# Up projection of the feed-forward part: 4 plain pairs of tiles, then 18 pairs by Strassen's seven products

## The reference

```python
def conv_ffn(h, w_up, conv_w, conv_b, w_down):     # D_FF = 2816, w_up is 1024 x 5632, w_down 2816 x 1024
    u = h @ w_up
    u_pad = jnp.pad(u, ((0, 0), (2, 0), (0, 0)))
    u = conv_b + conv_w[0] * u_pad[:, 0:s] + conv_w[1] * u_pad[:, 1:1 + s] + conv_w[2] * u_pad[:, 2:2 + s]
    gate, val = u[..., :D_FF], u[..., D_FF:]
    return (jax.nn.silu(gate) * val) @ w_down
# x = x + conv_ffn(rms_norm(x), ...), then a last rms_norm
```

## Time and profile before

| | us |
|---|---|
| three runs, median (lowest to highest) | 2477.18 (2477.11 to 2480.08) |
| profiled execution, its own time | 2477.57 |
| its span, first to last instruction | 2476.0 |
| TensorE busy | 2448.7 (99%), 11696 matmuls |
| VectorE busy | 1416.4 (57%) |
| ScalarE busy | 805.5 (33%) |

### The profile page before, as it was taken

The page is one execution under the profiler, slowest core; times in us unless marked ns, Lnnn a source line. Parts: engine busy times, 40 slices in busy tenths (PEclk is TensorE's granted clock), DMA queues, the critical chain, the costliest instruction groups (busy, mean ns, idle before and its releaser), DMA issues.

```text
span 2476.0 us, 31910 instructions
## 1 busy us (share of the span) xinstructions
PE 2448.7 (99%) x11696; PEld 2035.2 (82%) x11696; DVE 1416.4 (57%) x2288; ACT 805.5 (33%) x1513; POOL 95.4 (4%) x112
## 2 busy tenths in 40 slices
PE   8999999999999999999999999999999999999998
PEld 6888888888888888887788888988888888888876
DVE  5747887777532242435555743563677257734775
ACT  5334545444521131222233243452322112211224
POOL 1000000000000000021000030012000000000000
PEclk9999999999999999999999999999999999999999
DMA  5111111111111131221110142451111111111123
GB/s 198 35 43 52 43 52 50 45 51 52 51 51 43 50 119 47 80 85 48 42 47 22 30 141 85 132 192 51 43 51 51 44 50 51 48 46 51 46 62 122
DMA packets 236404, 160.97 MB, mean 65 GB/s; under 512 B 5295, under 2 KB 223572, under 8 KB 235299
## 3 DMA queue, kind: packets, MB, share of 16 engines
q1 hardware_dynamic: 229456, 132.66, 17.9%
q0 software_dynamic: 4976, 18.75, 2.2%
q10 hardware_dynamic: 1890, 8.43, 1.1%
HBM read 138.85 MB, written 20.97 MB: 65 GB/s over the span
## 4 chain that ended last, share of the span: by engine, by line
PE 97%; DVE 1%; DMA 1%; ACT 0%; issue 0%; SPq 0%; ACTq 0%; DVEq 0%
PE bank L716 26%; PE bank L717 26%; PE bank L718 26%; PE bank L1050 1%; PE bank L871 1%; PE bank L1051 1%; PE bank L1052 1%; PE bank L1247 1%; PE bank L1249 1%; PE bank L1248 1%; PE bank L1103 1%; PE bank L1104 1%; PE bank L1102 1%; DMA wraw<-in_w_in_dram 1%; PE bank L883 1%; PE bank L882 1%
## 5 line engine op out<-in xcount | busy, mean ns | idle before, releaser
L716 PE MATMUL bank<-xhi,whi 128*128 128x512 f32 x1056 | 411.8, 390 | 0.5 <-DVE wlo L1861 0.5
L717 PE MATMUL bank<-xlo,whi 128*128 128x512 f32 x1056 | 411.0, 389 | 0.0
L718 PE MATMUL bank<-xhi,wlo 128*128 128x512 f32 x1056 | 411.0, 389 | 0.0
L1861 DVE TENSOR_TENSOR wlo<-wraw,whi 128x1024 fp32r<-128x1024 f32 (+1 forms) x240 | 285.2, 1188 | 149.3 <-ACT whi L1281 99.8
L1288 ACT ACTIVATE whi<-wraw 128x1024 fp32r<-128x1024 f32 x132 | 139.3, 1056 | 573.2 <-PE bank L718 569.3
L716 PE MATMUL bank<-x4hi,whi 128*128 128x512 f32 x704 | 274.3, 390 | 0.0
L718 PE MATMUL bank<-x4hi,wlo 128*128 128x512 f32 x704 | 273.9, 389 | 0.0
L717 PE MATMUL bank<-x4lo,whi 128*128 128x512 f32 x704 | 273.9, 389 | 0.0
L716 PEld LDWEIGHTS bank<-xhi,whi 128*128 128x128 f32 x1056 | 198.3, 188 | 42.7 <-DVE wlo L1861 0.7
L717 PEld LDWEIGHTS bank<-xlo,whi 128*128 128x128 f32 x1056 | 198.3, 188 | 41.5 <-issue 0.2
L718 PEld LDWEIGHTS bank<-xhi,wlo 128*128 128x128 f32 x1056 | 198.3, 188 | 41.1
(11 more groups left out here) (397 smaller groups left out, 4507.2 us busy)
## 6 DMA issues: line engine op xcount, KB each, us to landing
wraw<-in_w_in_dram SPq DMA_DIRECT2D x85, 512.0 KB, 3.8
wraw<-in_ffn_w_up_dram SPq DMA_DIRECT2D x44, 512.0 KB, 3.7
wraw<-in_xattn_wkv_dram SPq DMA_DIRECT2D x16, 512.0 KB, 4.0
wraw<-in_ffn_w_down_dram SPq DMA_DIRECT2D x16, 512.0 KB, 3.9
wraw<-in_ffn_w_down_dram SPq DMA_DIRECT2D x16, 384.0 KB, 3.4
xraw<-in_x_dram SPq DMA_DIRECT2D x4, 1024.0 KB, 10.2
x_spill<-xt SPq DMA_DIRECT2D x8, 512.0 KB, 2.8
conv_spill<-tv POOLq DMA_DIRECT2D x8, 512.0 KB, 3.1
```

Of the source, the lines that this page charges most:

```text
L716: pe.matmul(acc, whi[slot][:, k, :], xh, start=(k == 0), stop=False)
L717: pe.matmul(acc, whi[slot][:, k, :], xl, start=False, stop=False)
L718: last = pe.matmul(acc, wlo[slot][:, k, :], xh, start=False, stop=(k == k_tiles - 1))
L1861: dve.tensor_tensor(wlo[slot][:, 0:n, :], wraw[slot][:, 0:n, :], whi[slot][:, 0:n, :].bitcast(F32), ALU.subtract).then_inc(s_wlo, 1)
```

## The change

The first 4 pairs stay plain matmuls. For each of the other 18, the product of [gate tile; value tile] with [tokens 0 to 511, tokens 512 to 1023], contraction in two halves of 4 blocks, is a product of 2 x 2 blocks, a11 a12 (gate), a21 a22 (value) by b11 b12, b21 b22, and is made with seven block products instead of eight (Winograd's form of Strassen):

- the weights' sums s1 = a21 + a22, s2 = s1 - a11, s3 = a11 - a21, s4 = a12 - s2 are made for each pair by VectorE (`weight_sum`), and seven high and low parts by ScalarE and VectorE (`weight_hi`, `weight_lo`) instead of two of double size;
- the input's sums t1 to t4 are made once, between the plain pairs (`t_forms`: terms on ScalarE, sums and low parts on VectorE);
- each product is 4 blocks x 3 matmuls of 512 columns. A pair uses three banks, x, y and z (`FORM_BANKS`: 4, 5, 6 or 0, 1, 2 in turn). ScalarE copies bank x to bank y before y is accumulated further (`y_begin`), copies y out (`copy_v`), and again (`copy_u3`); VectorE sums c12, c22 and takes c11, c21 times R.

Other parts: the first tap and SiLU move to ScalarE (`tap0`, `silu`). f tiles no longer stay in SBUF: each is stored to DRAM as it is made (`store_f`) and loaded again (`load_f`), and its two parts made then (`f_hi`, `f_lo`). All 22 pairs come first, then 8 + 8 down tiles, then the last 8 by half as before. The first down tile stands in banks 6 and 7. Some semaphores are shared.

```diff
+PLAIN = 4
+T_DN = T_FF + 2 * PLAIN
+T_LAST = T_DN + 16
+WEIGHT_ORDER = ("a11", "s1", "a12", "s2", "s3", "a22", "s4")
...
+            def next_pair(p, stored=None, last=False):            # SP
+                sp.wait_ge(s_as, 4 * p + 4)
+                sp.wait_ge(s_alo, 7 * p + 3)
...
+                    load_gate(p + 1)
+                if stored is not None:
+                    store_f(stored)
+                sp.wait_ge(s_alo, 7 * p + 6)
...
+                    load_value(p + 1)
...
+            for r, done in enumerate((2, 3, 5, 7)):
+                sp.wait_ge(s_m, 7 * LASTP + done)
+                for n in (2 * r, 2 * r + 1):
...
+                    load_f(n)
...
+            def form_step(p, q, first=False, last=False):         # TensorE
+                form_product("s1", "t1", "z", p, q)
+                pe.wait_ge(s_cp, 3 * p + 1)
+                form_product("s2", "t2", "y", p, q)
+                form_product("a12", "b21", "x", p, q)
+                pe.wait_ge(s_cp, 3 * p + 2)
+                form_product("s3", "t3", "y", p, q)
+                if not last:
+                    if not first:
+                        pe.wait_ge(s_c, 4 * p - 2)
+                    form_product("a11", "b11", "x", p + 1, 1 - q)
+                pe.wait_ge(s_cp, 3 * p + 3)
+                form_product("a22", "t4", "y", p, q, 2 if last else 1)
+                pe.wait_ge(s_c, 4 * p + 1)
+                form_product("s4", "b22", "z", p, q)
...
+            def first_down_tile():
...
+                for ks in (range(0, 6), range(6, 8)):
+                    for h in range(2):
+                        for k in ks:
+                            pe.wait_ge(s_ffn_lo, k + 1)
...
+            def form_step(p, q, first=False, last=False):         # ScalarE
+                weight_hi("s4", p)
+                if not last:
+                    weight_hi("a11", p + 1)
+                if not first:
+                    taps_of(p - 1)
+                copy_v(p, q)
+                if not last:
+                    weight_hi("s1", p + 1)
+                    weight_hi("a12", p + 1)
+                if not first:
+                    silu(p + (PLAIN - 1), 2)
+                if not last:
+                    weight_hi("s2", p + 1)
+                else:
+                    f_hi(0)
+                    f_hi(1)
+                copy_u3(p, q)
+                if not last:
+                    weight_hi("s3", p + 1)
+                    y_begin(p + 1, 1 - q)
+                    weight_hi("a22", p + 1)
...
+            def form_step(p, q, first=False, last=False):         # VectorE
+                n = p + (PLAIN - 1)
+                if not first:
+                    c12(p - 1, 1 - q)
+                    normed_hi(p - 1)
+                weight_lo("s4", p)
+                if not last:
+                    weight_lo("a11", p + 1)
+                if not first:
+                    taps(n, uv, yv, FF_TILES, 1)
+                if not last:
+                    weight_sum("s1", p + 1)
+                if not first:
+                    taps(n, ug, yg, 0, 2)
+                if not last:
+                    weight_sum("s2", p + 1)
+                    weight_lo("s1", p + 1)
+                    weight_sum("s4", p + 1)
+                    weight_lo("a12", p + 1)
+                else:
+                    f_lo(0)
+                    f_lo(1)
+                c22(p, q)
+                if not last:
+                    weight_sum("s3", p + 1)
+                    weight_lo("s2", p + 1)
+                if not first:
+                    product(n)
+                if not last:
+                    weight_lo("s3", p + 1)
+                else:
+                    f_lo(2)
+                    f_lo(3)
+                    split(T_DN, T_DN % 2)
+                    split(T_DN + 1, (T_DN + 1) % 2)
+                c11_c21(p, q)
+                if not last:
+                    weight_lo("a22", p + 1)
+                else:
+                    f_lo(4)
+                    f_lo(5)
...
+            def copy_u3(p, q):                                    # ScalarE
+                act.wait_ge(s_m, 7 * p + 5)
+                act.wait_ge(s_tap, 2 * p + (2 * PLAIN - (0 if isinstance(p, int) and p == 0 else 1)))
+                act.activation(uv[:, 2 + HALF:2 + S], ps(FORM_BANKS[q]["y"]), ACT.Copy).then_inc(s_cp, 1)
...
+            def c11_c21(p, q):                                    # VectorE
+                dve.wait_ge(s_m, 7 * p + 7)
...
-                        order.link(conv(i, yv, FF_TILES + done, h * HALF, HALF))
-                        dve.wait_ge(s_ffn_tanh, i * 2 + (2 * done + h + 1))
```

More of the change, by code:

```diff
@@ new lines, in _ @@
+            for n in range(PLAIN):
+                load(T_FF + 2 * n, G0, gate_of(n))
+                load(T_FF + 2 * n + 1, G1, gate_of(n + FF_TILES))
+                if n >= 2:
+                    store_f(n - 2)
+            sp.wait_ge(s_wlo, T_DN - 1)
+            load_gate(0)
+            sp.wait_ge(s_wlo, T_DN)
+            load_value(0)
+            store_f(PLAIN - 2)
+            next_pair(0, PLAIN - 1)
+            next_pair(1)
+            with sp.Fori(2, LASTP) as i:
+                next_pair(i, i + (PLAIN - 2))
@@ L578, in _ @@
+            load(T_DN + 3, (T_DN + 1) % 2, wd[:, :, 3, :])
+            loads(T_DN + 4, 4, (wd, 4, 2), (wd, 5, 2))
+            wd = tiles(ffn_w_down_2[0, 8 * P:16 * P, :])
+            loads(T_DN + 8, 8, (wd, 0, 2), (wd, 1, 2))
+            wd = tiles(ffn_w_down_2[0, 16 * P:FF_TILES * P, :])
+            for r in range(2):
+                loads(T_LAST + 8 * r, 8, (wd, 0, 2), (wd, 1, 2))
             out_v = out[0].rearrange("(b p) d -> p b d", p=P)
@@ new lines, in _, with form_product @@
+            mean_square(3)
+            dense(T_FF + 1, G1, x4hi, x4lo)
+            with pe.Fori(1, PLAIN) as i:
+                dense(2 * i + T_FF, G0, x4hi, x4lo)
+                dense(2 * i + (T_FF + 1), G1, x4hi, x4lo)
+            def form_product(a, b, to, p, q, inc=1):
+                onto = (a, b) not in (("a11", "b11"), ("s1", "t1"))
+                first = isinstance(p, int) and p == 0
+                pe.wait_ge(s_alo, 7 * p + (WEIGHT_ORDER.index(a) + 1))
+                o = ps(FORM_BANKS[q][to])
+                if first and b in t_at:
+                    pe.wait_ge(s_xlo, 36)
+                for k in range(HK):
+                    if first and b == "t4":
+                        pe.wait_ge(s_xlo, 36 + k + 1)
+                    xh, xl = form_of(b, k)
+                    pe.matmul(o, ahi[a][:, k, :], xh, start=(k == 0 and not onto), stop=False, skip_group_check=True)
+                    pe.matmul(o, ahi[a][:, k, :], xl, start=False, stop=False, skip_group_check=True)
+                    last = pe.matmul(o, alo[a][:, k, :], xh, start=False, stop=(k == HK - 1), skip_group_check=True)
+                last.then_inc(s_m, inc)
@@ new lines, in _ @@
+            weight_hi("s2", 0)
+            y_begin(0, 0)
+            weight_hi("s3", 0)
+            act.wait_ge(s_acc, 2 * T_DN)
+            for k in range(HK):
+                form_hi("t4", k, 3)
+            weight_hi("a22", 0)
+            form_step(0, 0, first=True)
+            with act.Fori(0, (LASTP - 1) // 2) as i:
+                form_step(2 * i + 1, 1)
+                form_step(2 * i + 2, 0)
+            form_step(LASTP, LASTP % 2, last=True)
+            f_hi(6)
+            f_hi(7)
@@ L1832, in _ @@
+            for n in range(8):
+                split(T_DN + n + 10, (T_DN + n) % 2)
+                if n < FF_GROUPS[-1]:
+                    f_hi(16 + n)
+                if n < 2:
+                    load_f(20 + n)
             for n in range(2 * KT):
@@ new lines, in _ @@
+            for k in range(HK):
+                form_lo("t4", k, 12 + k + 1)
+            weight_lo("a22", 0)
+            form_step(0, 0, first=True)
+            with dve.Fori(0, (LASTP - 1) // 2) as i:
+                order.enter(i, 4)
+                form_step(2 * i + 1, 1)
+                form_step(2 * i + 2, 0)
+                order.leave((LASTP - 1) // 2)
+            form_step(LASTP, LASTP % 2, last=True)
+            c12(LASTP, LASTP % 2)
+            f_lo(6)
+            f_lo(7)
@@ new lines, in _ @@
+            normed_hi(LASTP)
+            taps(FF_TILES - 1, uv, yv, FF_TILES, 1)
+            taps(FF_TILES - 1, ug, yg, 0, 2)
+            product(FF_TILES - 1)
+            for n in range(16):
+                t = T_DN + n
+                for h in range(2):
+                    dve.wait_ge(s_acc, 2 * t + h + 1)
+                    r = resid[:, n % KT, h * HALF:(h + 1) * HALF]
+                    dve.tensor_tensor(r, ps(6 + h if n == 0 else 2 * (t % 2) + h), r, ALU.add).then_inc(s_free, 1)
+                split(t + 2, t % 2)
+                if 8 + n < FF_TILES:
+                    f_lo(8 + n)
```

520 lines of the change are left out of this document (387 added, 133 removed).

## The result

The changed kernel took 2437.09 us (median of 4 runs, 2434.79 to 2438.04) beside 2478.53 us for the kernel before (4 runs, 2477.11 to 2480.08): a ratio of 0.9831, with a 95% interval of 0.9814 to 0.9848. A second comparison, of five runs of it and nine of the kernel before, gave 2438.06 against 2478.43, 0.9838 (0.9825 to 0.9852). The forecast was 2434.5. The profiled execution of the changed kernel took 2437.63 us with a span of 2435.8.

What follows compares the result with a forecast made beforehand. TensorE was taken to bound the kernel: 49.0 us of matmuls removed, 3.2 lost at the start and 3.1 at the end, so -42.7 us from 2477.57 and 0.4 for the median: 2434.5 us, range 2431 to 2453.

Steps and rivals of the forecast that it cites:

- What bounds the kernel: Changed part before the edit: TensorE is full, its longest wait 0.5 us, so time is matmuls times their 0.2268 us spacing.
- The matmuls taken away: Up projection, 18 pairs by products: each loses one product of 12 matmuls, 2.72 us, so 49.0 us less TensorE work.
- VectorE keeps up: Each step by products: VectorE's work takes 16.5 us of TensorE's 19.05, from start spacings in dense stretches.
- the dear end of 18.1: VectorE's work per step if operations do not overlap at all: 18.1 us, still under 19.05.
- the other dear end, 20.6: VectorE's work per step with no overlap plus a 0.14 us gap at 18 instructions: 20.6 us, over TensorE's step.
- The middle: The 16 steps between the first and the last: nothing waits on TensorE's side, 0 us lost.
- The start: First step by products: 3.2 us lost, 2.75 of it waiting for copy_u3 behind the next value tile's load.
- The end: Last step and first down tile: TensorE waits 1.4 for copy_u3, then 0.5, 0.75 and 0.5; together 3.1 us.
- A (VectorE bound): Rival, steps by products: VectorE becomes the bound, 17 us more at 20 us a step, 28 at 20.6; chance 0.16.
- B (a bubble at every product): Rival: each of a step's 7 products begins with a 0.1 us gap on TensorE, 12 us more; chance 0.05.
- C (the loop through the value tile's load): Rival: slow landing of the value tile sets the step, 15 us more at 8.8 us landing; chance 0.06, 0.03 slower than before.
- D: Rival: matmuls are not taken away, or a missed hand-over gives all freed time back, 2477 us; chance 0.03.

Runs made afterwards that it cites:

- e_plain12: The changed kernel with 12 plain pairs and 10 by products instead of 4 and 18: 2457.79 us, 0.992 of the kernel before.
- e_dup3: The changed kernel with VectorE making the low part of a22 four times in each of the 16 middle steps: 2445.06 us, ratio 0.9869 to before.
- e_fill: The changed kernel with 14 unused matmuls ahead of TensorE's wait for copy_v in the first step: 2435.89 us (one run).
- e_end: The changed kernel with the last step's ScalarE and VectorE work reordered, copy_u3 behind one high part of f instead of two: 2432.11 us (one run).

## Why the prediction was right, point by point

**What bounds the kernel.** Held, with one row misread: the 0.5 us of the earlier trace rows stands at 44 us into the program. In the changed part TensorE's longest wait before was 0.76 us, for `resid` at 2399 us, in the last down tiles. Nothing of the sum hangs on it.

**The matmuls taken away: 49.0 us.** Held. 216 fewer, and e_plain12 prices a pair at 2.6 us, 2.7 with its shorter first wait counted in. Steps of 19.04 us were forecast and are 19.04.

**VectorE keeps up: 16.5 us a step.** Held. It is busy for 16.6 us. Its round with the hand-overs is 17.26 us by e_dup3, so between the 16.5 taken and the dear end of 18.1; the other dear end, 20.6, was wrong: instructions in the loop with two waits and register arithmetic still start 0.60 us apart. The hand-worked step left 0.9 us spare behind c11_c21 and 0.8 were measured. It had the first value tap of VectorE's begin at 3.1 and sum s1 done at 6.4, which are 3.8 and 7.05 in the trace (1855.81 and 1859.05, less 1852.00): ScalarE's taps took 1.25 and 1.23 in place of 1.15, and two hand-overs, 0.45 and 0.15, were not counted. The sentence of "The DRAIN you can't avoid" that the prediction sets against its own spacing isn't all that this section of the Trainium skill's "VectorE: DVE Perf Modes" says: it adds that a next operation that isn't held starts earlier. The 0.60 in these steps, 0.08 less than a row of 0.68, agrees with that.

**ScalarE: 9.6 us.** 9.2 measured. SiLU was taken at 1.06 and is 1.063; the copies out of a bank were taken at 0.59 and are 0.57 to 0.60. A first tap was taken at 1.15 from x3hi's row, and is 1.24.

**The middle: no stall.** Held in all 16 steps.

**The start: 3.2 us, and 5.4 measured.** This is the step that failed. The prediction followed VectorE through "the low parts of t4, a22, s4 and a11 of the next pair" and found TensorE late by 0.4 for them, but it did not ask where a22's high part stands against copy_v in ScalarE's queue. By the slot's place it needs all of t4's low parts, and copy_v, for which s3's product waits, is three high parts behind it. By the prediction's own numbers it would have come out: t4's low parts end at 24.9 - 3 x 0.6 = 23.1, three high parts and the copy (4 x 0.58) bring copy_v to 25.4, and s3's product wants it one product ahead of 24.5, at 21.8: 3.6 us, where 3.14 were measured. The wait that was forecast, copy_u3 behind s1's high part and the value tile's load, was real: the load did land late, as worked out. It was hidden, since TensorE came there nearly 5 us later than thought, and e_fill brought it back at 0.2 us. Both have one pattern, later work ahead of a copy of the present product in ScalarE's queue. That 3.2 lies as near to 5.4 as it does is luck: the wait that made up 2.75 of it didn't occur, and one that was not seen did.

**The half clock: not forecast.** 1.4 us of the 5.4 by e_fill, 1.6 with the slow restart and the first matmul of the next product.

**The end: 3.1 us, and 3.15 measured.** The waits were found at the right places, and e_end shows their cause. Each was smaller than forecast (1.07, 0.38, 0.38, 0.17 against 1.4, 0.5, 0.75, 0.5): 2.0 us in all. The other 1.15 are late and slow restarts after each wait, which the prediction left out. That the two errors cancel is luck.

**Beside the plain pairs.** No wait of TensorE's stands there, as forecast.

**A (VectorE bound).** Did not happen, by 1.8 us a step. e_dup3 shows what it looks like: the two waits for TensorE vanish from VectorE's rows, and TensorE's losses are so small each (0.4 a step) that none of them heads the list of waits.

**B (a bubble at every product).** Did not happen: 285.66 us for 15 x 84 = 1260 matmuls is 0.2267 each, as in the earlier trace rows.

**C (the loop through the value tile's load), D.** Did not happen. The load took 3.7 us where 7.9 would have decided, with the DMA share at 0.26 in place of 0.16.

**The sum.** -49.0 + 3.2 + 3.1 = -42.7 forecast, -49.0 + 5.4 + 3.15 = -40.45 by the trace, -41.4 by the medians. The forecast was 2.6 us low: 1.3 of that is the kernel before, whose median was 2478.53 in this comparison and 2477.18 in the runs that the forecast started from, and 1.3 the change. By the trace the change was overrated by 1.9 (-40.8 in place of -42.7), 2.2 too much in the first step less the 0.4 from elsewhere; the 0.6 between the two is within the spread of the start.

## What to carry to other kernels

When matmuls are taken away on a kernel that TensorE bounds, the middle of the loop is a count and a check of the other engines' reserve; the errors are in the first and the last step, where preparation for what follows stands in a strict queue ahead of what the present step needs. For each wait of the bounding engine, list everything ahead of its releaser in the releaser's own queue, with the waits that each of these has, those for a buffer that shares its place included. Then put hand-overs of the current step first: here that took no instruction away and gave 5.8 us in the changed part.
